# The scan's side projection: the lower contraction half of each unit issued one unit later, and its two partial sums taken by two engines

## The chip, the cores and the metric

The kernel is one program on one core of one Trainium2 chip. The metric is the device time of one execution in microseconds; before the change it is 3687.72 us (median of three runs, 3677.84 to 3689.55). TensorE (PE) multiplies, VectorE (DVE) and ScalarE (ACT) take its results out of the accumulators in PSUM, GpSimd (POOL) helps with masks and stores, SyncE (SP) issues most loads.

## The reference, cut to what matters

The reference is three transformer layers in float32 over 256 latent tokens (and 256 context tokens) of width 2048: an even and an odd attention layer, and a last one with three branches (neighbourhood attention, pooling, an RWKV-7 recurrence), merged by gates. Two parts of the last layer meet in the stage that is changed. One is the recurrence, in both directions of time:

```python
def step(S, inp):
    rt, vt, wt, kt, at, bt = inp
    sa = jnp.einsum('bhij,bhj->bhi', S, at)
    S = S * wt[:, :, None, :] + sa[..., None] * bt[:, :, None, :] + vt[..., None] * kt[:, :, None, :]
    return S, jnp.einsum('bhij,bhj->bhi', S, rt)
```

The other is a plain product: the normed input (256 x 2048) times columns of the layer's input projection, which give the merge gates. It doesn't depend on the recurrence.

## The kernel before, in words

The program is a row of stages, and in each a large projection runs on TensorE beside some other work. Here that stage is `rwkv_scan`, name `scan`.

**The scan** is done in chunks: 16 heads in four groups `g`, each with four steps `s` of 128 tokens, so 16 rounds, the last two steps of each group with outputs ("lat"). Direction `d` is 0 or 1. TensorE makes in each round, for both directions, a fixed row of stages: `turned` (transposes), `products`, `half1`, `level1`, `av`, `half2`, `level2` and so on to `level5` (an inverse by doubling), `tz`, `outer`, `chain1`, `y` (lat only), `chain2`. One stage of one direction is a "visit", `visits` is the list of all 560. Behind most of them another engine works: VectorE adds or transposes (`ft`, `at`, `ak`, `t0`, `y1`, `t1`, ..., `pm`, `m1`, `m2`), ScalarE copies (`ft`, `rb_rk`, `tt0`, `tt1`, `av`, ..., `tz`, `outer`, `y`), GpSimd masks. Each engine has its order written out by loops over the same rounds, and `after` makes an engine wait for another's stage by a counting semaphore.

**The projection beside it** is class `Stream`. Its result is 16 tiles of 128 rows x 512 columns, each a sum over `KD` = 16 slices of 128 contraction rows. One slice is a *unit*: four products of 64 x 64 weights by 512 columns, one in each quadrant of TensorE's array (each is two instructions in the trace, so a unit has 8). Contraction rows 0 to 63 (index `r` = 0, the upper half) add into PSUM bank `ps[0]`, rows 64 to 127 (`r` = 1, the lower) into `ps[1]`. There is one pair of banks. The quadrants are taken in the order (0,0), (1,1), (0,1), (1,0) of (`r`, `o`), `o` being the half of the output rows, so two neighbours differ in both.

**The order.** `units_by(i)` says how many units TensorE has issued before visit `i`: 20 before the first, then shares by the table `share`. In the middle of the stage that is one unit behind each pair of visits of a stage (both directions), two behind `products`. `tiles_by(i)` = `units_by(i) // KD` places `sum_halves(v, t)` on VectorE: ahead of the first stage of VectorE whose visit comes after the tile's last unit. `evict(act, t)` on ScalarE comes six visits later.

When a tile is full, `sum_halves` waits for it and for a free stage buffer, copies `ps[0]` out (L3096), drains, adds `ps[1]` (L3098) and counts `summed`. The first unit of the next tile waits on TensorE for that count:

```python
            if t >= 1:
                pe.wait_ge(self.summed, t)
```

`evict` applies the activation in place (L3105) and issues the store. I call the change from tile `n`-1 to tile `n` *handover `n`*: unit 16`n`-1 ends a tile and unit 16`n` begins the next. There are 15. Where they lie in the order of TensorE, by `units_by`:

| Handover | Last unit issued behind | Visits between | First unit | Visits between | Second unit |
|---|---|---|---|---|---|
| 1 | (lead of 20 units) | none | 16 | none | 17 |
| 2 | level5 | tz | 32 | outer, chain1 | 33 |
| 3 | outer | chain1, chain2 | 48 | turned, products | 49 |
| 4 | chain2 | turned, products (lat) | 64 | none | 65 |
| 5 | products | none | 80 | half1 | 81 |
| 6 | products | half1 | 96 | level1 | 97 |
| 7 | level1 | av, half2 | 112 | level2 | 113 |
| 8 | half2 | level2 | 128 | half3 | 129 |
| 9 | level2 | half3 | 144 | level3 | 145 |
| 10 | half3 | level3 | 160 | half4 | 161 |
| 11 | half4 | level4 | 176 | half5 | 177 |
| 12 | level4 | half5 | 192 | level5 | 193 |
| 13 | half5 | level5 | 208 | tz | 209 |
| 14 | level5 | tz, outer | 224 | chain1, chain2 | 225 |
| 15 | chain1 | y, chain2 | 240 | turned, products | 241 |

SyncE loads weights (quarters of a chunk, six slots) and the scan's inputs; `load_after` decides which weight loads go ahead of which input loads. `store.tile_done` and `store.quarter_read` are counted by TensorE and free the weight slots.

## Time and profile before

| | |
|---|---|
| median of three runs | 3687.72 us (3677.84 to 3689.55) |
| profiled execution, its own time | 3688.84 us |
| its span in the profile | 3687.0 us |
| TensorE busy in the program | 3446.0 us (93%) |
| VectorE busy | 2038.0 us (55%) |
| ScalarE busy | 760.8 us (21%) |
| GpSimd busy | 562.8 us (15%) |
| the scan stage, from its first product to its last sum | 2785.6 to 3344.6 us |
| in it: the projection's 2048 product instructions, busy | 310.6 us, 605 ns mean |
| VectorE's 16 copies / 16 adds of the tiles | 687 / 688 ns mean |
| ScalarE's 16 in-place copies | 630 ns mean |

The span is the profiled execution's own, and lies 1.84 us below its time. Products of TensorE overlap, so a product's own duration is not what a unit costs; that is read from the distance of starts. "idle before" is time in which the engine did nothing, and what ended it.

### The profile page before, as it was taken

The numbers are of one execution on the slowest core, as the hardware profiler recorded it, in microseconds if no ns is written. First come the engines' busy times: TensorE is split into PE (matmuls) and PEld (weight loads), VectorE is DVE, ScalarE is ACT, GpSimd is POOL, SyncE is SP. The second block draws the span as 40 slices with busy tenths as digits, with TensorE's granted clock in tenths as the row PEclk, the third lists the DMA queues.
The fourth block names the chain that finished last, engine by engine and source line by source line (L and its number), as shares of the span: only waits on it lengthen the run. The fifth ranks groups of instructions, "written<-read, shape, count | busy, mean of one in ns | idle before, by whom it ended". The sixth has DMA issues, their size and how long they took to land. (4 is left out here: it accounts for less than half of the span.)

```text
span 3687.0 us, 54760 instructions
## 1 busy us (share of the span) xinstructions
PE 3446.0 (93%) x22059; PEld 1746.9 (47%) x22059; DVE 2038.0 (55%) x3206; ACT 760.8 (21%) x1543; POOL 562.8 (15%) x809
## 2 busy tenths in 40 slices
PE   6999998899989999899989999998899898899998
PEld 2354443334544446454444444454335666664443
DVE  1699992443346867556656647553653444444435
ACT  2100001121320112232110000033552333341000
POOL 0011111121000001100000010252212433432100
PEclk9999999999999999999999999999999999999999
DMA  9988995883245556426466676646875344336763
GB/s 365 346 304 309 355 379 196 321 312 128 74 147 205 182 192 229 167 85 249 167 235 227 245 282 249 240 132 222 279 245 191 114 131 154 118 116 208 238 209 114
DMA packets 362606, 798.66 MB, mean 217 GB/s; under 512 B 26631, under 2 KB 73791, under 8 KB 357747
## 3 DMA queue, kind: packets, MB, share of 16 engines
q1 hardware_dynamic: 259760, 459.54, 36.5%
q0 software_dynamic: 72992, 274.20, 20.7%
q10 hardware_dynamic: 29602, 61.42, 4.4%
q8 instruction: 176, 2.88, 0.3%
q14 instruction: 76, 0.61, 0.0%
HBM read 686.90 MB, written 108.18 MB: 216 GB/s over the span
## 5 line engine op out<-in xcount | busy, mean ns | idle before, releaser
L1228 PE MATMUL gemm_a_g_ps<-store_w,turned 128*128 128x512 f32 (+1 forms) x1152 | 457.2, 559 | 2.7 <-PEq L108 2.7
L759 DVE SCALAR_TENSOR_TENSOR pmods_acc<-pmods_w,cond,pmods_acc 128x512 f32<-128x512 f32 x540 | 384.4, 748 | 23.6 <-issue 0.5
L3084 PE MATMUL scan_g_ps<-store_w,turned 64*64 64x512 f32 x2048 | 310.6, 605 | 19.2 <-DVE outlet_stage L3098 12.3
L1228 PEld LDWEIGHTS gemm_a_g_ps<-store_w,turned 128*128 128x128 f32 x1152 | 209.2, 191 | 250.0 <-issue 250.0
L1228 PE MATMUL att_a_g_ps<-store_w,turned 128*128 128x512 f32 x512 | 240.2, 599 | 6.9 <-ACT outlet_stage L2812 4.2
L1228 PE MATMUL feat_g_ps<-store_w,turned 128*128 128x512 f32 x384 | 181.2, 621 | 15.9 <-ACT outlet_stage L2240 13.7
L1275 PE MATMUL out_c_g_ps<-store_w,turned 128*128 128x512 f32 x384 | 167.6, 592 | 0.0
L1228 PE MATMUL tail_g_ps<-store_w,tail_branch_t 128*128 128x512 f32 x384 | 165.8, 592 | 1.0 <-ACT tail_branch_t L3897 0.9
L1228 PEld LDWEIGHTS att_a_g_ps<-store_w,turned 128*128 128x128 f32 x512 | 91.5, 191 | 100.0 <-issue 93.4
L1228 PEld LDWEIGHTS feat_g_ps<-store_w,turned 128*128 128x128 f32 x384 | 73.2, 197 | 114.9 <-issue 96.0
L1307 DVE TENSOR_TENSOR store_w<-store_w 128x1024 f32<-128x1024 f32 (+1 forms) x108 | 121.1, 1179 | 0.0
L1275 PE MATMUL out_c_g_ps<-out_c_g_form,turned 128*128 128x512 f32 x272 | 118.9, 592 | 0.0
L1275 PEld LDWEIGHTS out_c_g_ps<-store_w,turned 128*128 128x128 f32 x384 | 72.8, 190 | 90.9 <-issue 90.9
L1228 PEld LDWEIGHTS tail_g_ps<-store_w,tail_branch_t 128*128 128x128 f32 x384 | 72.6, 190 | 90.8 <-issue 90.5
L3474 ACT ACTIVATE scan_tmt<-scan_ps 64x256 f32<-64x256 f32 (+1 forms) x224 | 85.1, 380 | 146.3 <-DVE scan_tm L3423 107.4
L1275 PE MATMUL gemm_hq_g_ps<-store_w,turned 128*128 128x512 f32 x256 | 111.2, 592 | 1.8 <-PEq L3972 1.8
L1275 PE MATMUL out_a_g_ps<-store_w,turned 128*128 128x512 f32 (+1 forms) x288 | 112.6, 546 | 0.0
L1275 PE MATMUL out_a_g_ps<-store_w,turned_c 128*128 128x512 f32 (+1 forms) x288 | 112.6, 545 | 0.0
L3084 PEld LDWEIGHTS scan_g_ps<-store_w,turned 64*64 64x64 f32 x2048 | 89.7, 133 | 45.7 <-issue 30.1
L1228 PE MATMUL lat_g_ps<-store_w,lat_turned 128*128 128x512 f32 x224 | 99.5, 603 | 10.8 <-ACT outlet_stage L2420 6.7
L1550 ACT ACTIVATE outlet_stage<-gemm_a_g_ps 128x512 f32<-128x512 f32 (+1 forms) x36 | 20.0, 555 | 433.4 <-PE gemm_a_g_ps L1228 433.4
L3308 PEld LDWEIGHTS scan_ps<-scan_tm,scan_lt 64*64 64x64 f32 x2560 | 77.2, 134 | 46.7 <-POOL scan_lt L3524 24.2
(577 smaller groups left out, 5807.5 us busy)
## 6 DMA issues: line engine op xcount, KB each, us to landing
store_w<-in_w_in SPq DMA_DIRECT2D x160, 1024.0 KB, 7.5
pmods_w<-in_w_mod POOLq DMA_DIRECT2D x40, 2048.0 KB, 13.3
store_w<-in_a_w_in SPq DMA_DIRECT2D x48, 1024.0 KB, 12.5
store_w<-in_c_w_in SPq DMA_DIRECT2D x40, 1024.0 KB, 8.2
first_mods_w<-in_w_mod SPq DMA_DIRECT2D x32, 1024.0 KB, 14.3
store_w<-in_a_w_out SPq DMA_DIRECT2D x32, 1024.0 KB, 6.1
scan_raw<-s_feat SPq DMA_DIRECT2D x112, 256.0 KB, 5.2
s_feat<-feat_o POOLq DMA_DIRECT2D x16, 1536.0 KB, 7.8
```

Source lines behind the costliest of these rows:

```text
L759: v.scalar_tensor_tensor(a, src, x, a, ALU.mult, ALU.add)
L1228: mm = pe.matmul(to, lhs, self.store.slot[i % self.store.NS][:, k, :width], start=first, stop=last)
L1275: mm = pe.matmul(self.pair_bank(n, product, j), act_tile(product, k, j), src[:, kk, :width], start=(k == 0), stop=(k == KT // 2 - 1))
L1307: v.tensor_tensor(w01, w11, w01, ALU.subtract).then_inc(store.piece_made, 1)
L1550: act.activation(outlet.stage[o % 4][:, :w.shape[1]], g.out(t), func).then_inc(copied, 1)
L3084: mm = pe.matmul(self.ps[r][halves[o], :], self.act_tile(k, tb)[halves[r], halves[o]], self.store.slot[i % self.store.NS][halves[r], k % 4 ...
L3308: mm = pe.matmul(quarter(d, 2, 0)[turned_chunk(d, c), h, :], lt[d][chunks[c], k - 1, h, :], tm[d][chunks[c], h, :], start=True, stop=True)
L3474: act.activation(dst, src, ACT.Copy)
```

## The change

TensorE still issues four quadrant products per unit, but the two lower ones are those of the unit before. The new `product(pe, r, o, n)` issues one quadrant product of unit `n`; slot `n` of the order now holds (0,0) of `n`, (1,1) of `n`-1, (0,1) of `n`, (1,0) of `n`-1. Slot 0 has only its two upper products, and the last slot has the two lower products of its own unit behind it. So bank `ps[0]` of a tile is full one slot before bank `ps[1]`.

The handover is split. ScalarE copies `ps[0]` to the stage buffer (`take_upper`) when `upper_done` says that it is full, and counts `upper_taken`; slot 16`n` waits for that. VectorE then only adds `ps[1]` (`sum_halves`) and counts `summed`; slot 16`n`+1 waits for that. `take_upper` stands on ScalarE ahead of the first stage whose visit comes after the tile's last upper products; `sum_halves` on VectorE is placed by `tiles_by` = `(units_by(i) - 1) // KD`, and so is `evict`. `load_after` counts one unit more before a slot of weights is free.

```diff
@@ -3048,7 +3048,8 @@
         self.tiles = [(c, j) for c, job in enumerate(projections) for j in range(len(job[1]))]
         self.out_of = outlet.take(len(self.tiles))
         self.ps = [st.enter_context(nc.psum_tensor(f"{name}_ps{r}", [P, NCH], F32)) for r in range(2)]
-        self.summed, self.evicted = [nc.alloc_semaphore(f"{name}_{s}") for s in ("summed", "evicted")]
+        self.upper_done, self.upper_taken, self.summed, self.evicted = [
+            nc.alloc_semaphore(f"{name}_{s}") for s in ("upper_done", "upper_taken", "summed", "evicted")]
 
     def wait_tile(self, eng, t):
 
@@ -3063,38 +3064,71 @@
         end = begin = self.store.load_of[self.base]
         while end < self.store.load_of[self.base + len(self.projections)] + self.store.NS:
             old, part = (end - self.store.NS - begin) // 4, (end - self.store.NS - begin) % 4
-            if old >= 0 and 2 * KD * old + KD + 4 * (part + 1) > n_units:
+            if old >= 0 and min(2 * KD * old + KD + 4 * (part + 1) + 1, len(self.tiles) * KD) > n_units:
                 break
             end += 1
         self.store.load(sp, end)
 
+    def product(self, pe, r, o, n):
+
+        t, k = n // KD, n % KD
+        c, j = self.tiles[t]
+        i = self.store.load_of[self.base + c] + k // 4
+        halves = (slice(0, HD), slice(HD, P))
+        return pe.matmul(self.ps[r][halves[o], :], self.act_tile(k, self.projections[c][1][j])[halves[r], halves[o]],
+                         self.store.slot[i % self.store.NS][halves[r], k % 4, :], start=(k == 0), stop=(k == KD - 1))
+
     def units(self, pe):
 
-        for t, (c, j) in enumerate(self.tiles):
-            tbs = self.projections[c][1]
-            tb = tbs[j]
-            if t >= 1:
-                pe.wait_ge(self.summed, t)
-            halves = (slice(0, HD), slice(HD, P))
-            for k in range(KD):
-                i = self.store.load_of[self.base + c] + k // 4
-                if j == 0 and k % 4 == 0:
-                    self.store.wait_quarter(pe, i)
-                for r, o in ((0, 0), (1, 1), (0, 1), (1, 0)):
-                    mm = pe.matmul(self.ps[r][halves[o], :], self.act_tile(k, tb)[halves[r], halves[o]],
-                                   self.store.slot[i % self.store.NS][halves[r], k % 4, :], start=(k == 0), stop=(k == KD - 1))
-                if k == KD - 1:
-                    mm.then_inc(self.store.tile_done, 1)
-                elif k % 4 == 3 and j == len(tbs) - 1:
-                    mm.then_inc(self.store.quarter_read, 1)
-                yield
+        def upper_ready(n):
+            t, k = n // KD, n % KD
+            c, j = self.tiles[t]
+            if k == 0 and t >= 1:
+                pe.wait_ge(self.upper_taken, t)
+            if j == 0 and k % 4 == 0:
+                self.store.wait_quarter(pe, self.store.load_of[self.base + c] + k // 4)
+
+        def lower_ready(n):
+            if n % KD == 0 and n >= KD:
+                pe.wait_ge(self.summed, n // KD)
+
+        def upper_finished(mm, n):
+            if n % KD == KD - 1:
+                mm.then_inc(self.upper_done, 1)
+
+        def lower_finished(mm, n):
+            t, k = n // KD, n % KD
+            c, j = self.tiles[t]
+            if k == KD - 1:
+                mm.then_inc(self.store.tile_done, 1)
+            elif k % 4 == 3 and j == len(self.projections[c][1]) - 1:
+                mm.then_inc(self.store.quarter_read, 1)
+        last = len(self.tiles) * KD - 1
+        for n in range(last + 1):
+            upper_ready(n)
+            if n:
+                lower_ready(n - 1)
+            self.product(pe, 0, 0, n)
+            if n:
+                self.product(pe, 1, 1, n - 1)
+            upper_finished(self.product(pe, 0, 1, n), n)
+            if n:
+                lower_finished(self.product(pe, 1, 0, n - 1), n - 1)
+            if n == last:
+                self.product(pe, 1, 1, n)
+                lower_finished(self.product(pe, 1, 0, n), n)
+            yield
+
+    def take_upper(self, act, t):
+
+        self.outlet.wait_free(act, self.out_of + t)
+        act.wait_ge(self.upper_done, t + 1)
+        act.activation(self.stage(t), self.ps[0][:, :], ACT.Copy).then_inc(self.upper_taken, 1)
 
     def sum_halves(self, v, t):
 
-        self.outlet.wait_free(v, self.out_of + t)
+        v.wait_ge(self.upper_taken, t + 1)
         self.wait_tile(v, t)
-        v.tensor_copy(self.stage(t), self.ps[0][:, :])
-        v.drain()
         v.tensor_tensor(self.stage(t), self.stage(t), self.ps[1][:, :], ALU.add).then_inc(self.summed, 1)
 
     def evict(self, act, t):
@@ -3179,9 +3213,13 @@
 
             return lead + (n_units - lead) * room[i // 2] // room[-1]
 
+        def uppers_by(i):
+
+            return units_by(i) // KD
+
         def tiles_by(i):
 
-            return units_by(i) // KD
+            return max(0, units_by(i) - 1) // KD
 
         def mask(d, i):
             return masks[:, d, i, :].unsqueeze(1).broadcast_to([P, HG, HD])
@@ -3501,14 +3539,21 @@
             for k in levels[:-1]:
                 run[f"tt{k}"] = copies(f"level{k}", lambda d, lat, x: swapped(d, tmt[d][:, :, :], quarter(d, 0, 0)), f"t{k}")
             run[f"tt{N_LEVELS}"] = copies(f"level{N_LEVELS}", lambda d, lat, x: [(tmt[d][:, :, :], quarter(d, 0, 0))])
-            t = 0
+            made_by = {"ft": "turned", "rb_rk": "products", "tt0": "products"}
+            t = taken = 0
             for g, s in rounds:
                 for stage in stages("act", steps[s][2]):
                     for d in range(2):
-                        while t < tiles_by(max(0, visit_of[(g, s, {"ft": "turned", "rb_rk": "products", "tt0": "products"}.get(stage, stage.replace("tt", "level")), d)] - 6)):
+                        visit = visit_of[(g, s, made_by.get(stage, stage.replace("tt", "level")), d)]
+                        while taken < uppers_by(visit):
+                            gemm_side.take_upper(act, taken)
+                            taken += 1
+                        while t < tiles_by(max(0, visit - 6)):
                             gemm_side.evict(act, t)
                             t += 1
                         run[stage](d, g, s, steps[s][2])
+            for rest in range(taken, len(gemm_side.tiles)):
+                gemm_side.take_upper(act, rest)
             for rest in range(t, len(gemm_side.tiles)):
                 gemm_side.evict(act, rest)
```

The order of VectorE at handover 4 (round g 0, s 3; `outlet_stage` is the stage buffer, `scan_g_ps` the two banks). Before, the copy and the add stand ahead of the two copies of the transposed inputs (`scan_ft`):

```order
L3438 TENSOR_TENSOR scan_m<-scan_ps,scan_m 64x256 x4
L3096 COPY outlet_stage<-scan_g_ps 128x512
L3098 TENSOR_TENSOR outlet_stage<-outlet_stage,scan_g_ps 128x512
L3397 COPY scan_ft<-scan_ps 128x512 x2
L3402 TENSOR_TENSOR scan_tmt<-scan_ps,scan_masks 128x2x2x64
L3403 TENSOR_TENSOR scan_at<-scan_ps,scan_masks 128x2x2x64
L3402 TENSOR_TENSOR scan_q<-scan_ps,scan_masks 128x2x2x64
L3403 TENSOR_TENSOR scan_at<-scan_ps,scan_masks 128x2x2x64
L3412 TENSOR_TENSOR scan_akt<-scan_ps,scan_masks 128x2x2x64
L3409 STREAM_TRANSPOSE scan_tm<-scan_tmt 128x256
L3412 TENSOR_TENSOR scan_akt<-scan_ps,scan_masks 128x2x2x64
L3409 STREAM_TRANSPOSE scan_tm<-scan_q 128x256
```

Of the change:

```order
L3476 TENSOR_TENSOR scan_m<-scan_ps,scan_m 64x256 x4
L3435 COPY scan_ft<-scan_ps 128x512 x2
L3440 TENSOR_TENSOR scan_tmt<-scan_ps,scan_masks 128x2x2x64
L3441 TENSOR_TENSOR scan_at<-scan_ps,scan_masks 128x2x2x64
L3440 TENSOR_TENSOR scan_q<-scan_ps,scan_masks 128x2x2x64
L3441 TENSOR_TENSOR scan_at<-scan_ps,scan_masks 128x2x2x64
L3450 TENSOR_TENSOR scan_akt<-scan_ps,scan_masks 128x2x2x64
L3447 STREAM_TRANSPOSE scan_tm<-scan_tmt 128x256
L3450 TENSOR_TENSOR scan_akt<-scan_ps,scan_masks 128x2x2x64
L3447 STREAM_TRANSPOSE scan_tm<-scan_q 128x256
L3132 TENSOR_TENSOR outlet_stage<-outlet_stage,scan_g_ps 128x512
L3455 TENSOR_TENSOR scan_y<-scan_ps,scan_eye 128x256 x2
```

The copy is gone, and the add has moved from ahead of `ft` to behind the two transposes `scan_tm` of `t0`: bank `ps[1]` is now full at the end of slot 64, which TensorE issues behind `products`. Slot 65, which follows slot 64 with nothing between, waits on TensorE for this add.

The order of ScalarE at handover 9. The rows are the copies of `av` (`scan_raw`), of level 2 and of level 3 (`scan_tmt`, one row for direction 0 and one for direction 1 each). Before, the projection has its in-place copy behind level 3:

```order
L3474 ACTIVATE scan_raw_0<-scan_ps 128x256
L3474 ACTIVATE scan_raw_1<-scan_ps 64x256 x2
L3474 ACTIVATE scan_tmt<-scan_ps 128x256
L3474 ACTIVATE scan_tmt<-scan_ps 64x256 x2
L3474 ACTIVATE scan_tmt<-scan_ps 128x256
L3474 ACTIVATE scan_tmt<-scan_ps 64x256 x2
L3105 ACTIVATE outlet_stage<-outlet_stage 128x512
L1154 DMA s_merge<-outlet_stage 128x512
```

Of the change:

```order
L3512 ACTIVATE scan_raw_0<-scan_ps 128x256
L3512 ACTIVATE scan_raw_1<-scan_ps 64x256 x2
L3512 ACTIVATE scan_tmt<-scan_ps 128x256
L3512 ACTIVATE scan_tmt<-scan_ps 64x256 x2
L3126 ACTIVATE outlet_stage<-scan_g_ps 128x512
L3512 ACTIVATE scan_tmt<-scan_ps 128x256
L3512 ACTIVATE scan_tmt<-scan_ps 64x256 x2
L3512 ACTIVATE scan_tmt<-scan_ps 128x256
L3512 ACTIVATE scan_tmt<-scan_ps 64x256 x2
```

The new copy out of the bank stands behind the copies of level 2 for both directions and ahead of level 3's.

## Rows read from the trace of the kernel before

**Rows 1.** The page's head.

```profile
span 3687.0 us, 54760 instructions
```

**Rows 2.** Windows: PE, PEld, DVE, ACT, POOL busy, granted clock, DMA; the scan stage.

```profile
2785.00:3345.00 560.00, 503.24 (x13280) 363.02 (x13280) 246.53 (x584) 205.19 (x497) 207.24 (x304) 0.99 0.43 133
```

**Rows 3.** Waits in the scan stage: total us, times, longest.

```profile
PE scan_g_ps L3084 <- DVE outlet_stage L3098: 12.3, 11, 3.4
```

**Rows 4.** Timeline, first handover; start us, us, engine line op.

```profile
2799.68 0.69 DVE L3096 COPY outlet_stage<-scan_g_ps 128x512 f32<-128x512 f32 x1 [4.26 <-PE scan_g_ps L3084]
...
2801.19 2.38 PE L3084 MATMUL scan_g_ps<-store_w,turned 64*64 64x512 f32 x20 [1.64 <-DVE outlet_stage L3098]
```

**Rows 5.** Timeline at handover 10, in level 3 and half 4.

```profile
3121.82 0.75 PE L3308 MATMUL scan_ps<-scan_tm,scan_lt 64*64 64x64 f32 x26
...
3123.26 0.93 PE L3320 MATMUL scan_ps<-scan_tmt,scan_y 64*64 64x64 f32 x32
...
3123.72 0.69 DVE L3096 COPY outlet_stage<-scan_g_ps 128x512 f32<-128x512 f32 x1 [0.47 <-PE scan_g_ps L3084]
...
3125.23 1.09 PE L3084 MATMUL scan_g_ps<-store_w,turned 64*64 64x512 f32 x8 [1.04 <-DVE outlet_stage L3098]
...
3126.14 0.75 PE L3308 MATMUL scan_ps<-scan_tm,scan_lt 64*64 64x64 f32 x26
```

**Rows 6.** Timeline at handover 9, behind level 2.

```profile
3091.36 0.93 PE L3308 MATMUL scan_ps<-scan_tm,scan_lt 64*64 64x64 f32 x32
...
3091.67 0.77 ACT L3474 ACTIVATE scan_tmt<-scan_ps 64x256 f32<-64x256 f32 x2 [0.16 <-issue]
...
3093.33 1.09 PE L3084 MATMUL scan_g_ps<-store_w,turned 64*64 64x512 f32 x8 [1.05 <-DVE outlet_stage L3098]
```

**Rows 7.** Timeline: both copying engines take the two banks of a turned product.

```profile
2868.93 0.60 ACT L3474 ACTIVATE scan_ft<-scan_ps 128x512 f32<-128x512 f32 x1 [5.56 <-PE scan_ps L3269]
2868.93 0.69 DVE L3397 COPY scan_ft<-scan_ps 128x512 f32<-128x512 f32 x1 [1.46 <-PE scan_ps L3269]
```

**Rows 8.** Timeline at handover 2, beside tz.

```profile
2825.79 1.54 PE L3329 MATMUL scan_ps<-scan_raw,scan_tmt 64*64 64x128 f32 x32
...
2826.88 1.89 ACT L3474 ACTIVATE scan_tz<-scan_ps 128x512 f32<-128x512 f32 x3 [0.99 <-PE scan_ps L3329]
...
2827.77 1.09 PE L3084 MATMUL scan_g_ps<-store_w,turned 64*64 64x512 f32 x8 [0.44 <-DVE outlet_stage L3098]
```

**Rows 9.** Timeline at handover 3, between chain 1 and chain 2.

```profile
2865.88 0.95 PE L3359 MATMUL scan_ps<-scan_m,scan_pm 64*64 64x64 f32 x13 [1.34 <-DVE scan_m L3438]
```

**Rows 10.** Timeline behind handover 4: `ft`, last transpose, first unit behind half 1.

```profile
2906.95 1.28 DVE L3397 COPY scan_ft<-scan_ps 128x512 f32<-128x512 f32 x2
...
2911.91 0.45 DVE L3409 STREAM_TRANSPOSE scan_tm<-scan_q 128x256 f32<-128x256 f32 x1
...
2912.91 0.65 PE L3084 MATMUL scan_g_ps<-store_w,turned 64*64 64x512 f32 x2
```

**Rows 11.** Timeline at handover 5, behind products of a first round.

```profile
2946.73 0.84 ACT L3474 ACTIVATE scan_tmt<-scan_q 64x256 f32<-64x256 f32 x2 [3.94 <-DVE scan_tm L3409]
...
2948.10 1.09 PE L3084 MATMUL scan_g_ps<-store_w,turned 64*64 64x512 f32 x8 [3.39 <-DVE outlet_stage L3098]
```

**Rows 12.** Timeline at handover 7, beside av and half 2.

```profile
3014.19 0.77 ACT L3474 ACTIVATE scan_tmt<-scan_ps 64x256 f32<-64x256 f32 x2 [0.16 <-issue]
...
3015.86 1.09 PE L3084 MATMUL scan_g_ps<-store_w,turned 64*64 64x512 f32 x8 [0.47 <-DVE outlet_stage L3098]
```

**Rows 13.** Timeline from the stage's end to the next stage's first product.

```profile
3344.66 0.63 ACT L3105 ACTIVATE outlet_stage<-outlet_stage 128x512 f32<-128x512 f32 x1 [3.38 <-DVE outlet_stage L3098]
...
3346.84 3.75 PE L1275 MATMUL tail_g_ps<-store_w,turned 128*128 128x512 f32 x4 [3.79 <-PEq L3972]
```

**Rows 14.** Windows round two long idle stretches of TensorE (columns of Rows 2).

```profile
2940.00:2950.00 10.00, 6.48 (x137) 3.80 (x133) 7.16 (x17) 1.60 (x4) 9.09 (x15) 1.00 0.29 81
...
3066.00:3072.00 6.00, 6.00 (x138) 4.73 (x139) 0.00 (x0) 2.54 (x5) 0.00 (x0) 0.72 0.16 49
```

## The prediction

> **What bounds the kernel now.** I read the page's head first: the span is 3687.0 us [rows 1], and the profiled execution's own time is 3688.84 us, 1.1 above the median of 3687.72. Then the stretch of the scan stage, the only one that the change touches: in 560 us TensorE is busy for 503.2, VectorE for 246.5, ScalarE for 205.2 [rows 2]. So the stage is TensorE's, and both other engines have room; what they do costs time only where TensorE waits for it. Third the waits: the projection's units stand idle for 12.3 us, 11 times, until VectorE's add [rows 3]. That is the wait that the change splits. Last the timeline at each handover, for what it costs and what would come in its place.
>
> The plain case is handover 10 [rows 5]. From one pair of visits to the next, with one unit between, it is 3123.26 - 3121.82 = 1.44 us. Across the handover it is 3126.14 - 3123.26 = 2.88. So a handover costs 1.44 us. A unit alone takes 3126.14 - 3125.23 = 0.91, hence a pair of visits 0.53. The copy starts 0.46 after the last unit's end (3123.72 against 3123.26, where TensorE goes on), and the unit starts at 3125.23, 0.05 after copy and add (0.69 each, 0.08 between) have ended. The wait's length is latency and serial work, 0.46 + 0.69 + 0.08 + 0.69 + 0.05 = 1.97, less the 0.53 of visits that cover it.
>
> **The change, part by part.** It removes 16 copies and drains on VectorE and adds 16 copies on ScalarE. VectorE and ScalarE start on the banks of one turned product at the same 2868.93 and take 0.69 and 0.60 [rows 7], so I give the new copy 0.60 and the same 0.46 and 0.05 round it. ScalarE's path is then 0.46 + 0.60 + 0.05 = 1.11 us from the unit's end (*upper wait*), and VectorE's 0.46 + 0.69 + 0.05 = 1.20 from the end of the next slot (*lower wait*). Both are longer than the 0.53 of one pair of visits. The single wait of 1.44 becomes two: 1.11 - 0.53 = 0.58, then 1.20 - 0.53 = 0.67. That is the point of the forecast: two short paths, each with its own latency, stand one behind the other, since in most of the stage one slot lies between two pairs of visits. By handover:
>
> - 8, 10, 11 (last unit behind a half): 0.58 + 0.67 = 1.25 against 1.44, -0.2 each, -0.6.
> - 9, 12 (behind a level): ScalarE must first finish the level's copies, from 3091.67 for 0.77 to 3092.44 [rows 6]; the new copy stands behind them (the order of ScalarE above), ends at 3093.1, and the slot starts at 3093.15 against 3093.33 now. It gains 0.2, the lower wait adds 0.67: +0.5 each, +1.0.
> - 13: upper wait 0.58; the lower is covered by tz, a pair that takes about 1.97 - 0.8 = 1.2 (next line). 0.6 against 1.44: -0.8.
> - 2: the unit starts at 2827.77, where the path of 1.97 from 2825.79 ends [rows 8]. TensorE's idle time there is 0.44, to which the tail of the last modelled product adds some 0.36, so the cost is 0.8. ScalarE's copy would run from 2826.25 to 2826.85, beside tz, and be out of the way as ScalarE's own tz copy starts at 2826.88. Both waits go: -0.8.
> - 3: the sum stands ahead of `m1`, and chain 2 waits 1.34 for it [rows 9]; both halves of it now lie where TensorE has other work: -1.3.
> - 14: free now. The add moves between `pm` and `m1`, behind slot 224; `m1` can start 1.15 after that slot (0.46 + 0.69) in place of about 0.28 + 0.41 = 0.69 (half a pair of visits, and the latency): +0.5.
> - 15: covered before and after, 0.
> - 4: the new order's worst place. The add, now behind `t0`, holds slot 65. The last transpose ends at 2911.91 + 0.45 = 2912.36 [rows 10]; as the sum no longer holds up `ft` (2906.95), all of it comes some 0.4 earlier (0 to 0.69 possible). Add and latency end at 2912.7, slot 65 at 2913.6, the pair of half 1 at 2914.1, where it now ends at 2912.91: +1.2.
> - 5: the unit waits 3.39 us now, and starts at 2948.10 [rows 11]. ScalarE's copy stands behind its `tt0`, which ends at 2946.73 + 0.84 = 2947.57; plus 0.03, 0.60 and 0.05 is 2948.25, +0.15. Then the lower wait, +0.67. +0.8. Handover 6 has the same order behind `products`: +0.8.
> - 7: ScalarE's copy follows 3014.19 + 0.77 = 3014.96 and lets the slot start at 3015.6 against 3015.86 [rows 12], -0.25; lower wait +0.67: +0.4.
> - 1: no visits between. 1.97 now (2801.19 less 2799.68 is 1.51, plus the 0.46) [rows 4]; 1.11 + 1.20 after: +0.35.
>
> Sum: -0.6 + 1.0 - 0.8 - 0.8 - 1.3 + 0.5 + 1.2 + 0.8 + 0.8 + 0.4 + 0.35 = +1.55.
>
> **The ends.** Slot 0 holds half a unit and takes at most a whole one's time, so the lead of 20 slots doesn't grow (it may lose 0.45). At the end the two lower products of unit 255 stand alone, 0.45 to 0.9. TensorE isn't what ends the stage: its next product starts at 3346.84, after ScalarE's last in-place copy from 3344.66 [rows 13]. From unit 255's end that chain has 0.46 + 0.69 + 0.08 + 0.69 = 1.92 now; then 0.9 + 0.46 + 0.69 = 2.05, the upper copy being done beside. +0.1.
>
> **What else moves.** The 11 us of copies (16 x 0.69) that leave VectorE buy nothing by themselves, as it is idle for over half of the stage [rows 2]; where its queue counted (3, 4) it is priced above. ScalarE gets 16 x 0.60 = 9.6 us; behind `take_upper` stand its own stage copies. In the plain rows these are due two stages later, and at handover 2 the copy fits in the gap by 0.03; were that gone it would cost 0.1. Freed weight slots come one slot later, and no unit waits for weights in the waits of this stage; SyncE's rule shifts by the same one, so its input loads aren't held. The products are the same 2048.
>
> Total +1.65 us on 3688.84 is 3690.5; against the median, 3687.72 + 1.65 = **3689.4 us**. A measurement of this kernel can tell about 0.3% (11 us) from no change; this is 0.04%. Each latency has bounds: were ScalarE's path 0.3 shorter or longer at 15 handovers, the sum would run from -3 to +6.
>
> **Rivals.**
>
> *Both waits hidden.* If ScalarE and VectorE each got their bank out under the visits, all of what handovers cost now would go: six of 1.44, 1.97, 0.8, 1.3, 0.4, 3.4, 0.9 and 0.85, some 18 us: 3670. For it: both engines are idle for over half of the stage. Against it: 1.11 and 1.20 against a cover of 0.53. 0.06. Here the Trainium skill speaks for the change: "TensorEngine Tiling (Array Packing)", section PSUM Bottleneck, advises to use ScalarE and VectorE both to empty PSUM. By it the time would be this rival's. The rows show a wait made of latencies, not of throughput.
>
> *More waits, lower clock (slower).* Where TensorE idles, its clock may fall to the lower level. Behind an idle stretch that ended at 3065.96 it shows 0.72 of full over 6 us [rows 14], so 1.7 us lost; but round the 3.39 us ahead of unit 80 it stayed at 1.00, and the stage has 0.99 with its 11 waits [rows 2, 11, 14]. About 12 lower waits are new. From six such falls on (6 x 1.7 = 10, with the 1.65) it is slower by over 0.3%; all 12 give 3689.4 + 20 = 3710. 0.05. The Trainium skill has this as a rule, "TensorE: Matmul & The Clock Gate", section on psum-queue depth-cycling: a kernel that cycles through PSUM banks with short idle times between groups makes the clock swing. The trace disagrees so far, by that 0.99.
>
> *Quadrants that no longer read the same slice (slower).* Neighbouring products of a slot now stream slices of two units. No row shows such a pair. If it cost 0.04 us a unit, 256 x 0.04 = 10 us would decide; a unit whose four quadrants ran one by one would double to 1.8, +230. The nearest row is the unit itself, which already streams from different partitions for the two halves, so I take 0. 0.03.
>
> *Drift.* The three runs lie 11.7 us apart, and the instructions behind the edit move in memory; TensorE's idle stretches that no engine released are in the same stage. Within the range; a little of it lies beyond 0.3% on either side, 0.03 and 0.03.
>
> **How the numbers follow.** Forecast and drift within 0.3%: 0.80, plus 0.01 for the clock case in its mild form. Faster 0.09 (0.06 + 0.03), slower 0.10 (0.04 + 0.03 + 0.03). The range is the forecast with the spread of the runs, 13 below and 11 above: 3676 to 3700; the two far cases lie outside.
>
> **What would show it.** In the profile after: ScalarE's 16 new copies at 0.60 us; TensorE's units waiting for ScalarE at some 11 handovers (0.6 us, longest 3.4 at handover 5) and again for VectorE at some 11 (0.7, longest about 2.7 at handover 4); no wait of chain 2 at handover 3; a stage of 560 us within 3; a granted clock of 0.99. A pair-to-pair distance other than 1.44 away from handovers would show the quadrant rival, a lower clock the second, and units that wait for VectorE less than 4 us in all the first.

## The result, and the profile after

The changed kernel takes 3692.18 us (median of 20 runs, 3685.30 to 3696.23), the kernel before 3685.07 (20 runs, 3677.84 to 3696.25). The ratio is 1.0018, with a 95% interval of 1.0012 to 1.0024: slower by 4.4 to 8.8 us. I had forecast +1.65. One execution of the kernel before in the comparisons told below took 6304.35 us at a granted clock of 0.677; the ratios leave it out.

The page's head of the kernel after (the profiled execution's own time is 3691.34 us):

```profile
span 3689.6 us, 54760 instructions
```

Its windows, of the same 560 us (columns as in [rows 2]):

```profile
2785.00:3345.00 560.00, 502.17 (x13207) 364.46 (x13205) 234.38 (x565) 213.26 (x510) 203.38 (x298) 0.98 0.42 130
```

Against [rows 2] VectorE has lost 12 us (234.38 for 246.53) and ScalarE gained 8 (213.26 for 205.19), about what 16 instructions of 0.69 and 0.60 make. TensorE gets 1 us less done in the same stretch, and its granted clock is 0.98 for 0.99.

The waits of TensorE there (columns as in [rows 3]):

```profile
PE scan_g_ps L3078 <- ACT outlet_stage L3126: 7.6, 7, 3.7
...
PE scan_g_ps L3078 <- DVE outlet_stage L3132: 3.2, 2, 2.3
```

12.3 us in 11 waits [rows 3] have become 7.6 in 7 for ScalarE and 3.2 in 2 for VectorE, 10.8 in all. The sum of waits fell by 1.5 us and the time rose. Short waits are missing from this view, since they hide under a product's modelled end (handover 10, below, shows no idle time). So I also went by starts.

The view of the stage buffer, with how long its instructions take (ns: shortest, median, longest):

```profile
L3126 ACT ACTIVATE outlet_stage<-scan_g_ps x15: 597/597/599, 2795.7 to 3307.9; 128x512 f32<-128x512 f32 x15
L3132 DVE TENSOR_TENSOR outlet_stage<-outlet_stage,scan_g_ps x15: 649/689/689, 2797.6 to 3311.1; 128x512 f32<-128x512 f32 x15
```

The new copy takes 0.60 us, as I had put it.

The timeline at handover 10, which answers to [rows 5]:

```profile
3123.99 0.90 PE L3346 MATMUL scan_ps<-scan_tm,scan_lt 64*64 64x64 f32 x27
...
3125.59 0.92 PE L3358 MATMUL scan_ps<-scan_tmt,scan_y 64*64 64x64 f32 x32
...
3125.96 0.60 ACT L3126 ACTIVATE outlet_stage<-scan_g_ps 128x512 f32<-128x512 f32 x1 [0.89 <-PE scan_g_ps L3078]
...
3126.61 1.09 PE L3078 MATMUL scan_g_ps<-store_w,turned 64*64 64x512 f32 x8
...
3127.52 0.93 PE L3346 MATMUL scan_ps<-scan_tm,scan_lt 64*64 64x64 f32 x32
...
3127.84 0.69 DVE L3132 TENSOR_TENSOR outlet_stage<-outlet_stage,scan_g_ps 128x512 f32<-128x512 f32 x1 [0.79 <-PE scan_g_ps L3078]
...
3128.58 1.09 PE L3078 MATMUL scan_g_ps<-store_w,turned 64*64 64x512 f32 x8
...
3129.49 0.75 PE L3358 MATMUL scan_ps<-scan_tmt,scan_y 64*64 64x64 f32 x26
...
3130.94 0.75 PE L3346 MATMUL scan_ps<-scan_tm,scan_lt 64*64 64x64 f32 x26
```

Away from the handover, pair to pair is 3130.94 - 3129.49 = 1.45 us, as before (1.44). Slot 160 starts 1.02 after the end of the unit ahead (3126.61 - 3125.59), and slot 161 1.97 after slot 160 (3128.58 - 3126.61), where 1.45 would be no wait. From pair 3125.59 to pair 3129.49 it is 3.90 for two slots, 1.00 more than 2 x 1.45. Before, the one slot with the handover took 2.88, 1.44 too much. So this handover gains 0.4, where I had -0.2.

The timeline at handover 4, which answers to [rows 10]:

```profile
2902.19 1.04 PE L3078 MATMUL scan_g_ps<-store_w,turned 64*64 64x512 f32 x8
...
2904.50 0.45 DVE L3447 STREAM_TRANSPOSE scan_tm<-scan_q 128x256 f32<-128x256 f32 x1
...
2904.86 0.65 DVE L3132 TENSOR_TENSOR outlet_stage<-outlet_stage,scan_g_ps 128x512 f32<-128x512 f32 x1
...
2905.57 1.09 PE L3078 MATMUL scan_g_ps<-store_w,turned 64*64 64x512 f32 x8 [2.34 <-DVE outlet_stage L3132]
```

The add stands behind the last transpose, and slot 65 waits 2.34 us for it, as forecast (3.38 from start to start; 0.86 before).

At handover 5 ([rows 11] before), the first execution of the kernel after:

```profile
2938.49 1.04 PE L3078 MATMUL scan_g_ps<-store_w,turned 64*64 64x512 f32 x8
...
2941.08 0.45 DVE L3447 STREAM_TRANSPOSE scan_tm<-scan_q 128x256 f32<-128x256 f32 x1 [0.16 <-POOL scan_q L3568]
2941.56 0.84 ACT L3512 ACTIVATE scan_tmt<-scan_q 64x256 f32<-64x256 f32 x2 [3.94 <-DVE scan_tm L3447]
...
2942.56 0.60 ACT L3126 ACTIVATE outlet_stage<-scan_g_ps 128x512 f32<-128x512 f32 x1 [0.16 <-issue]
...
2943.21 1.99 PE L3078 MATMUL scan_g_ps<-store_w,turned 64*64 64x512 f32 x8 [3.67 <-ACT outlet_stage L3126]
...
2944.97 1.30 PE L3346 MATMUL scan_ps<-scan_tm,scan_lt 64*64 64x64 f32 x28
...
2945.33 0.69 DVE L3132 TENSOR_TENSOR outlet_stage<-outlet_stage,scan_g_ps 128x512 f32<-128x512 f32 x1 [3.80 <-PE scan_g_ps L3078]
```

ScalarE stands idle from 2937.6 to 2941.56 (3.94, for VectorE's transpose), and the copy stands behind `tt0`, though the bank was full some 3 us earlier (slot 79 starts at 2938.49 and takes 1.04). Slot 80 starts after 3.67 us of idle time, where [rows 11] had 3.39. Then something the sum did not have: its eight products take 1.99 us, where they took 1.09 in [rows 11]. That is the lower level of the clock, 1.2 GHz (the granted clock stands below). The same at handover 6:

```profile
2978.58 0.84 ACT L3512 ACTIVATE scan_tmt<-scan_q 64x256 f32<-64x256 f32 x2 [4.61 <-DVE scan_tm L3447]
...
2979.58 0.60 ACT L3126 ACTIVATE outlet_stage<-scan_g_ps 128x512 f32<-128x512 f32 x1 [0.15 <-issue]
...
2980.23 1.99 PE L3078 MATMUL scan_g_ps<-store_w,turned 64*64 64x512 f32 x8 [0.74 <-ACT outlet_stage L3126]
...
2982.35 0.69 DVE L3132 TENSOR_TENSOR outlet_stage<-outlet_stage,scan_g_ps 128x512 f32<-128x512 f32 x1 [2.39 <-PE scan_g_ps L3078]
```

The idle time just ahead is only 0.74 (TensorE had stood idle for 0.55 and 0.35 us more in the 3 us before it), and the products again take 1.99. The windows of the kernel after round both places (in the kernel before, [rows 14] has 1.00 round handover 5):

```profile
2943.00:2949.00 6.00, 5.79 (x116) 3.67 (x118) 2.24 (x5) 0.80 (x3) 5.57 (x9) 0.74 0.01 3
2977.00:2983.00 6.00, 4.36 (x70) 2.67 (x68) 2.83 (x7) 1.43 (x3) 6.00 (x10) 0.77 0.73 255
```

The same for the kernel before:

```profile
2948.00:2954.00 6.00, 5.90 (x164) 4.11 (x165) 2.34 (x7) 1.94 (x6) 5.75 (x9) 1.00 0.21 61
2981.00:2987.00 6.00, 5.74 (x160) 4.02 (x162) 3.08 (x9) 2.91 (x7) 5.93 (x9) 1.00 0.77 249
```

The granted clock, third from the end, is 0.74 and 0.77 after, 1.00 and 1.00 before.

The other waits that the prediction named: chain 2 at handover 3, 1.34 us before [rows 9]. In the waits of TensorE after, its line has left

```profile
PE scan_ps L3397 <- DVE scan_m L3476: 0.7, 3, 0.2
```

so that wait is gone, as forecast.

**All fifteen.** For each handover `n` the time from the start of slot 16`n`-1 to that of slot 16`n`+2 holds both waits. Of two profiled executions of the kernel before, three of the changed one, and four of variants told below:

```
handover   sum had   before         changed               early_h5 early_h6 copy_early skew_vector
 1         +0.35     4.47   4.47    5.12   5.12   5.12     5.12    5.12     5.12      5.23
 2         -0.8     10.36  10.36    9.68   9.69   9.69     9.68    9.68     9.69      9.68
 3         -1.3      9.92  11.54    8.81   8.81   8.81     8.81    8.81     8.81      9.14
 4         +1.2      8.71   8.72    9.82   9.82   9.82     9.82   10.65     9.82     11.04
 5         +0.8      7.32   8.94    9.02   9.38  10.27     5.22    9.35     5.22      7.08
 6         +0.8      7.24   7.24    9.20   9.17   8.04     8.04    7.06     7.05      7.06
 7         +0.4      5.78   5.78    6.21   6.21   6.21     6.21    6.21     6.21      5.59
 9         +0.5      5.78   5.78    6.21   6.21   6.21     6.21    6.21     6.21      5.51
10         -0.2      5.77   5.76    5.35   5.35   5.35     5.35    5.35     5.35      5.45
11         -0.2      5.77   5.78    5.40   5.40   5.40     5.40    5.40     5.40      5.51
15          0        8.86   8.86    8.86   8.86   8.86     8.86    8.86     8.86      8.93
```

Handovers 8, 12, 13 and 14 are left out: idle stretches of 1 to 3 us that no engine releases fall into them in some executions. Together they take 38.7 and 39.0 us before and 37.7, 38.7 and 40.0 in the changed kernel, the same in the mean. The nine quiet rows (all here but 5 and 6) sum to 65.44 in the first execution of the kernel before and 65.47 to 65.48 in the changed one: +0.03, where my terms give -0.05. The second execution of the kernel before has 67.05, since its clock fell at handover 3 (11.54 for 9.92); the 10.65 and 11.04 at handover 4 have a fall too. Rows 5 and 6 sum to 14.56 and 16.18 before, 18.22, 18.55 and 18.31 after: +3.0 between the means, where I had +1.6.

### The profile page after: what moved, and what is told of

Its sections match the earlier page's. It is cut to its first block and busy times, and to the rows that moved or that the text cites. A ratio compares the mean times of both kernels' runs of the same rounds, so it can differ in the third digit from the quotient of the medians.

```text
span 3689.6 us, 54760 instructions
## 1 busy us (share of the span) xinstructions
PE 3449.3 (93%) x22059; PEld 1751.7 (47%) x22059; DVE 2027.6 (55%) x3190; ACT 770.2 (21%) x1559; POOL 562.8 (15%) x809
## 3 DMA queue, kind: packets, MB, share of 16 engines
q8 instruction: 176, 2.88, 0.3%
## 5 line engine op out<-in xcount | busy, mean ns | idle before, releaser
L1228 PE MATMUL lat_g_ps<-store_w,lat_turned 128*128 128x512 f32 x224 | 100.5, 608 | 10.8 <-ACT outlet_stage L2420 6.7
```

Of the source, the lines that this page charges most:

```text
L1228: mm = pe.matmul(to, lhs, self.store.slot[i % self.store.NS][:, k, :width], start=first, stop=last)
```

## The experiments

Three groups of runs, each with the kernel before in turn on the same chip, whose medians there were 3686.78 (35 runs), 3685.90 (27) and 3688.06 (35).

**First group: is it the order, the second engine, or the two waits?**

*again*: the changed kernel once more, with no edit.

> The changed kernel once more, for a second profile beside the first. In the first its scan stage lasts 569.5 us against 561.3 before, of which 3.3 us lie at the handovers' two slots and 4.9 us elsewhere: more stretches in which TensorE stands idle with no engine behind it, and six falls of its granted clock in place of two. If these belong to the changed kernel, the stage is again 567 to 571 us, with five or more falls at the same slots; if they are chance of one execution, they lie at other slots and the stage may be 563 to 566 us. Against before: slower by 4 to 9 us, as the twenty runs have it.

Measured: 3693.18 us (12 runs), ratio 1.0015 (1.0006 to 1.0024). The loss repeats. The stage took 568.7 us with seven falls of the clock, and four of the first profile's six stand at the same slots (handovers 5 and 6, slots 120 and 254): in part the kernel's, in part chance.

*before_no_handover*: the kernel before, whose TensorE never waits at a handover. Copy and add read other data of the same size, so the projection's result doesn't reach the output.

```diff
-            if t >= 1:
-                pe.wait_ge(self.summed, t)
...
-        v.tensor_copy(self.stage(t), self.ps[0][:, :])
+        v.tensor_copy(self.stage(t), self.read[:, 0:NCH])
...
-        v.tensor_tensor(self.stage(t), self.stage(t), self.ps[1][:, :], ALU.add).then_inc(self.summed, 1)
+        v.tensor_tensor(self.stage(t), self.stage(t), self.read[:, NCH:2 * NCH], ALU.add).then_inc(self.summed, 1)
```

> The kernel before, with VectorE's copy and add reading from SBUF in place of the two banks, and TensorE never waiting for them; loads of all engines stay. It prices all 15 handovers. By my sum they cost 18 us (six of 1.44, 1.97, 0.8, 1.3, 0.4, 3.4, 0.9, 0.85): faster than before by 15 to 20 us. If handovers only shift idle time that TensorE would have anyway, under 8 us.

Measured: 3676.37 us (12 runs), ratio 0.9969 (0.9959 to 0.9979).

*after_no_handover*: the same with the changed kernel, both waits gone.

```diff
-            if k == 0 and t >= 1:
-                pe.wait_ge(self.upper_taken, t)
...
-            if n % KD == 0 and n >= KD:
-                pe.wait_ge(self.summed, n // KD)
+            return
...
-        act.activation(self.stage(t), self.ps[0][:, :], ACT.Copy).then_inc(self.upper_taken, 1)
+        act.activation(self.stage(t), self.read[:, 0:NCH], ACT.Copy).then_inc(self.upper_taken, 1)
...
-        v.tensor_tensor(self.stage(t), self.stage(t), self.ps[1][:, :], ALU.add).then_inc(self.summed, 1)
+        v.tensor_tensor(self.stage(t), self.stage(t), self.read[:, NCH:2 * NCH], ALU.add).then_inc(self.summed, 1)
```

> The changed kernel with both its handover waits and its reads of the banks taken away in the same manner (ScalarE and VectorE still work on data in SBUF). Theory 1, the loss is in the waits and what they do to the clock: this kernel equals the one before without handovers within 2 us. Theory 2, the loss is in the changed order of the products itself or in how the instructions reach TensorE: it is 4 to 6 us slower than that one.

Measured: 3675.78 us (12 runs), ratio 0.9975 (0.9963 to 0.9987). Without handovers the changed order is not slower (0.9969 and 0.9975, intervals that overlap). So streaming two slices in one slot costs nothing that shows within the some 4 us that these runs can tell, and the loss comes with the handovers. Taking all handovers away gains some 10 us net in the kernel before, and not the 18 that I had put in the first rival. Where the handover holds nothing up, TensorE meets VectorE, whose copy and add still stand ahead of the scan's own work, one stage later: in before_no_handover slot 161 comes 2.24 us after slot 160 (1.45 in the kernel before), since a transpose stands behind copy and add. The waits of TensorE there have a line for such transposes, which the kernel before doesn't have:

```profile
PE scan_ps L3307 <- DVE scan_tm L3422: 3.3, 3, 2.6
```

The 10 us is a rough price, for the copy that reads the other data is not the old one. It takes 0.43 us in place of 0.69, and 2.51 once, at handover 8, which makes the 2.6 in that line:

```profile
L3094 DVE COPY outlet_stage<-turned x16: 426/429/2509, 2797.9 to 3333.4; 128x512 f32<-128x512 f32 x16
```

In after_no_handover one add takes 4.93 us (at 3013.71), and TensorE waits 4.11 for the transpose behind it. What stretched the two was not tested. That profile is also of the slowest of its 12 executions, 3689.92 us.

*both_copy*: the kernel before without the skew; ScalarE copies the upper bank to the stage buffer and VectorE the lower one to a buffer of its own, at the same time, and the add comes two stages later from there.

```diff
             if t >= 1:
-                pe.wait_ge(self.summed, t)
+                pe.wait_ge(self.upper_taken, t)
+                pe.wait_ge(self.lower_taken, t)
...
+        act.activation(self.stage(t), self.ps[0][:, :], ACT.Copy).then_inc(self.upper_taken, 1)
...
+        v.tensor_copy(self.lower[:, :], self.ps[1][:, :]).then_inc(self.lower_taken, 1)
...
+        v.tensor_tensor(self.stage(t), self.stage(t), self.lower[:, :], ALU.add).then_inc(self.summed, 1)
```

> The kernel before (no skew), but at a handover ScalarE copies the upper bank to the stage buffer while VectorE copies the lower one to a buffer of its own in SBUF, and the add comes two stages later from SBUF. TensorE's path is then 0.46 + the longer of 0.60 and 0.69 + 0.05 = 1.20 us in place of 1.97: 0.77 less at handovers behind a half or without cover, 0.2 less behind a level, where ScalarE comes 1.1 us late. Sum about -7 us against before: faster by 4 to 9 us. If the clock or idle time elsewhere takes it back, within 2 us of before.

Measured: 3686.60 us (12 runs), ratio 0.9999 (0.9989 to 1.0009); the 4 to 9 us that I expected didn't come. A plain handover is shorter (10: 4.97 us in place of 5.77 before), but handover 5 takes 9.20, since ScalarE's copy stands behind `tt0` there too and the clock falls behind it. The waits show both:

```profile
PE scan_g_ps L3087 <- ACT outlet_stage L3099: 7.0, 6, 3.7
...
PE scan_g_ps L3087 <- DVE scan_g_lower L3104: 1.2, 2, 0.9
```

**Second group: ScalarE's place in its queue.** A new theory: the loss is at handovers 5 and 6, where `take_upper` stands behind `tt0`.

*copy_early*: the changed kernel with the copy ahead of `tt0` at these two.

```diff
-                        while taken < uppers_by(visit):
+                        early = visit_of[(g, s, "products", 1)] + 1 if stage in ("rb_rk", "tt0") else visit
+                        while taken < uppers_by(early):
```

> The changed kernel with one thing moved: at handovers 5 and 6 ScalarE's copy of the upper bank stands ahead of its tt0 copies in place of behind them. If the part of the loss that I had not priced (about 4 to 5 us of some 6.5) comes from these two places, where TensorE's clock fell in both profiles of the changed kernel: no fall of the clock at them, slots 80 and 81 together in 4 us in place of 6.7 to 7.6, and 3 to 5 us less than the changed kernel, so 1 to 4 us slower than before. If they play no part beyond their waits in the trace: about 2.5 us less. If the loss lies elsewhere: unchanged, 5 to 7 us slower than before.

Measured: 3686.82 us (11 runs), ratio 1.0001 (0.9992 to 1.0010). The loss is gone, with two of ScalarE's 1559 instructions moved. By its rows 5 and 6 (12.27 us, for 14.56 and 16.18 before) the kernel should even be faster than the one before, by some 3 us, and it isn't; that is taken up under what stays open.

*skew_vector*: the changed kernel with its order and its two waits, but VectorE takes both banks.

```diff
-        act.activation(self.stage(t), self.ps[0][:, :], ACT.Copy).then_inc(self.upper_taken, 1)
+        v.tensor_copy(self.stage(t), self.ps[0][:, :]).then_inc(self.upper_taken, 1)
...
+                    while taken < uppers_by(visit_of[(g, s, made_by.get(stage, stage), d)]):
+                        while t < taken:
+                            gemm_side.sum_halves(v, t)
+                            t += 1
+                        gemm_side.take_upper(v, taken)
+                        taken += 1
```

> The changed kernel's order of products and its two waits, but VectorE does both, the copy of the upper bank and the add of the lower; ScalarE is as before. If ScalarE's lateness matters (behind a level 0.6 us each at handovers 9 and 12, and at 5 and 6 its tt0 copies, 0.8 each) this is 3 to 4 us faster than the changed kernel; behind a half it is 0.1 slower each. If only the number of waits in a row matters, it equals the changed kernel within 1 us.

Measured: 3686.14 us (11 runs), ratio 1.0001 (0.9992 to 1.0010). Two waits as such don't cost the 6 us either. VectorE's copy at handover 5 lets slot 80 start after 2.62 us of idle time, since it doesn't stand behind `tt0`, and its products take 1.09:

```profile
2943.91 0.65 DVE L3126 COPY outlet_stage<-scan_g_ps 128x512 f32<-128x512 f32 x1
...
2944.62 1.09 PE L3078 MATMUL scan_g_ps<-store_w,turned 64*64 64x512 f32 x8 [2.62 <-DVE outlet_stage L3126]
```

*both_early*: both_copy with the two early places.

```diff
-                    while t < tiles_by(visit_of[(g, s, made_by.get(stage, stage), d)]):
+                    early = visit_of[(g, s, made_by.get(stage, stage), d)] + ((stage, d) == ("ak", 1))
+                    while t < tiles_by(early):
                         gemm_side.take_lower(v, t)
...
-                        while taken < tiles_by(visit):
+                        early = visit_of[(g, s, "products", 1)] + 1 if stage in ("rb_rk", "tt0") else visit
+                        while taken < tiles_by(early):
```

> The kernel in which both engines copy a bank each, with both copies of handovers 5 and 6 placed earlier (ScalarE's ahead of tt0, VectorE's ahead of the second ak). Slot 80 starts 1.5 us earlier and slot 96 about 0.5: 2 us faster than both_copy, so 2 us faster than before where that one was equal, and up to 8 if the whole gain worked out for it came. If TensorE gives the gain back by waiting for its own instructions, again within 1 us of before.

Measured: 3684.19 us (11 runs), ratio 0.9995 (0.9987 to 1.0004). The lowest median of all complete kernels, but not to be told from the kernel before.

*before_again*: the kernel before, for a second profile.

> The kernel before, for a second profile. Theory: with its one wait per handover its clock does not fall at handovers 5 and 6, and its stage lasts 559 to 564 us with two to four falls in all. If a fall stands at one of them here too, those falls are chance and not the change's.

Measured: 3686.97 us, span 3685.0. It moved my reading. Handover 5 takes 8.94 us here and 7.32 in the first profile; ahead of it TensorE is idle for 3.40 us (first profile 3.39), and this time the clock falls:

```profile
2948.31 1.58 PE L3084 MATMUL scan_g_ps<-store_w,turned 64*64 64x512 f32 x8 [3.40 <-DVE outlet_stage L3098]
```

```profile
2948.00:2954.00 6.00, 5.69 (x100) 3.58 (x102) 1.89 (x5) 0.38 (x1) 5.96 (x9) 0.72 0.01 3
```

0.72, where the first profile has 1.00 in the same stretch. The 1.00 in [rows 14], on which the prediction leaned, was one of two outcomes.

**Third group: the two places apart.**

*early_h5* and *early_h6*: copy_early for handover 5 alone and for 6 alone (`(g, s)` = (1, 0) and (1, 1)).

```diff
-                        early = visit_of[(g, s, "products", 1)] + 1 if stage in ("rb_rk", "tt0") else visit
+                        early = visit_of[(g, s, "products", 1)] + 1 if (g, s) == (1, 0) and stage in ("rb_rk", "tt0") else visit
```

> The changed kernel with ScalarE's copy of the upper bank ahead of tt0 at handover 5 alone. Theory: the loss is the local one at these two handovers. From the starts in the profiles, slots 80 to 82 took 4.71 + 1.97 + 2.70 = 9.38 us in the changed kernel and 1.80 + 1.97 + 1.45 = 5.22 with the copy early, 4.2 less; so this kernel is about 4 us below the changed one, ratio to the kernel before 1.0006 to 1.0009. Slot 80 starts 1.8 us behind slot 79, and slot 82 1.45 behind slot 81. Rival (the two matter only together, by the clock that falls at both): no gain or the whole one, 1.0017 or 1.0001. Rival (what copy_early gained was how its build happened to lie in memory): nothing follows the number of copies moved, any value from 0.9995 to 1.002.

> The changed kernel with ScalarE's copy of the upper bank ahead of tt0 at handover 6 alone. Theory: slots 96 and 97 took 4.04 + 2.87 us in the changed kernel and 2.91 + 2.11 with the copy early, 1.9 less; so this kernel is about 2 us below the changed one, ratio to the kernel before 1.0011 to 1.0013, and handover 5 shows its 4.71 and the half clock behind it as before. Rival (only together): 1.0017 or 1.0001. Rival (memory): any value from 0.9995 to 1.002, in no order with early_h5.

*copy_early_again* and *changed_third*, with no further edit:

> Copy_early once more, in the same call as its two halves. Theory: ratio to the kernel before 1.0000 to 1.0004, 6 us below the changed kernel, and the stage without a fall of the granted clock at handovers 5 and 6. Rival (chance): above 1.0010.

> The changed kernel in the same call as the three above: ratio 1.0015 to 1.0020, slots 80 and 96 at 4.71 and 4.04 us behind the slot before, granted clock fallen at both places. The gains of early_h5 and early_h6, taken from this run, should add up to that of copy_early_again, about 4 + 2 = 6 us.

Measured, 12 runs each: changed_third 3690.06 us, ratio 1.0011 (0.9999 to 1.0022); early_h6 3689.23, 1.001 (1.0 to 1.002); early_h5 3685.70, 1.0 (0.999 to 1.001); copy_early_again 3686.07, 0.9997 (0.9985 to 1.0008). From the changed kernel's median that is -0.8, -4.4 and -4.0 us. By the table's rows 5 and 6 the three should gain 1.9 (early_h6, 16.41 for a mean of 18.36), 5.1 (early_h5, 13.26) and 6.1 (12.27). Moving the copy at handover 5 alone takes the loss away, so the rival by which both places matter only together falls. The rival of memory is left with little: of the changed kernel's own order, the two programs with that copy moved (copy_early, twice, and early_h5) are level with the kernel before, and the two with it behind `tt0` (the changed kernel, three times, and early_h6) are not. For handover 6 the slots show about 1.0 of gain without the clock and the time can't tell it from 0; that the two gains add up was not shown. The changed kernel's own ratio is at the low end here: -0.4 to 8.1 us, where the first two comparisons have 4.4 to 8.8 and 2.2 to 8.8.

Handover 5 of early_h5:

```profile
2943.00 1.04 PE L3078 MATMUL scan_g_ps<-store_w,turned 64*64 64x512 f32 x8
...
2944.16 0.60 ACT L3126 ACTIVATE outlet_stage<-scan_g_ps 128x512 f32<-128x512 f32 x1 [2.03 <-PE scan_g_ps L3078]
...
2944.80 1.09 PE L3078 MATMUL scan_g_ps<-store_w,turned 64*64 64x512 f32 x8 [0.76 <-ACT outlet_stage L3126]
...
2946.03 0.69 DVE L3132 TENSOR_TENSOR outlet_stage<-outlet_stage,scan_g_ps 128x512 f32<-128x512 f32 x1
2946.07 0.84 ACT L3512 ACTIVATE scan_tmt<-scan_q 64x256 f32<-64x256 f32 x2 [1.32 <-DVE scan_tm L3447]
```

```profile
2944.00:2950.00 6.00, 5.24 (x136) 3.57 (x134) 3.95 (x10) 2.36 (x6) 6.00 (x10) 1.00 0.32 96
2977.00:2983.00 6.00, 5.13 (x134) 3.51 (x136) 2.35 (x7) 3.04 (x8) 6.00 (x9) 1.00 0.74 235
```

The copy starts soon after the bank is full, slot 80 waits 0.76 us in place of 3.67, `tt0` (2946.07) isn't held up, and the clock stays at 1.00 at both handovers.

## Why the prediction was right, and where it was not

"Within 0.3%" held, and the kernel landed in the range. The size did not: +1.65 against 4.4 to 8.8. Of the signs that I had set, two failed: the stage was to take 560 us within 3 and took 569.5, 568.7 and 565.9 (561.3 and 559.5 before), and the granted clock of 0.99 was 0.98.

**Pair to pair away from handovers** stayed at 1.45. The quadrant rival, slower by mixed slices, didn't come: by that distance, and by the two kernels without handovers.

**The two waits one behind the other** (the point of the forecast) is what the timeline shows. The sizes were a little high: I had 0.58 and 0.67 for upper and lower, and measured 1.93 - 1.45 = 0.48 and 1.97 - 1.45 = 0.52. The latency that I took from the old handover, 0.46, is 0.37 for ScalarE (3125.96 - 3125.59) and 0.32 for VectorE (3127.84 - 3127.52) in the rows of handover 10. Hence -0.4 for 10 and 11, not -0.2. Behind a level, 9 and 7, +0.43 each against +0.5 and +0.4.

**Handovers 1, 2, 3, 4, 15**: +0.65, -0.68, -1.11, +1.11 and 0, against +0.35, -0.8, -1.3, +1.2 and 0. At 1 the two waits don't follow the sum by 0.3; the rest is right within 0.2. Handovers 8, 12, 13 and 14 can't be read off single executions; their sum is unchanged, as forecast (-0.2 + 0.5 - 0.8 + 0.5 = 0).

**The step that failed: handovers 5 and 6, "+0.8 each"**, through the clock. Where the clock doesn't fall, 0.8 is right for both, in part by luck: the upper wait grew by 0.28 (4.71 for 4.43 at 5, 4.04 for 3.76 at 6) where I had 0.15, the lower is 0.52 where I had 0.67. At 6 the third execution of the changed kernel has 8.04 against 7.24. At 5, slot 80 starts 4.71 after slot 79 in all three (before 4.43), and slot 81 follows 1.97 us behind it where the clock holds; with 1.45 for slot 82 that is 8.13 against 7.32. But the clock fell at handover 5 in all three executions (and in early_h6, with the same 3.67 us of idle time), and at 6 in two of the three, which makes 8.13 into 9.02 to 10.27 and 8.04 into 9.2. In the kernel before it fell at 5 in one execution of two, 7.32 into 8.94, and at 6 in neither. That is 2.2 us against 0.8 between the means, +1.4, the whole of the gap between +1.6 and +3.0. The prediction priced the clock at nothing there: "round the 3.39 us ahead of unit 80 it stayed at 1.00". The rival "more waits, lower clock" came true in this mild form, to which I gave 0.01. I had priced a fall at 1.7 us; at these two places one cost 0.9 to 2.1. Its strong form, a fall at each of 12 new lower waits, did not come: the slots behind the short waits at 7, 9, 10 and 11 keep their lengths in every execution. Up to the next stage's first product I count 6, 7 and 4 falls in the changed kernel against 3 and 4 before, but the 12 that don't stand at handovers 5 and 6 all go with idle stretches of 1.4 to 3.5 us that no engine releases. The new wait of 2.34 us at handover 4, which I had priced at the full clock too, was followed by a fall in three of the eight executions that have it, though in none of the changed kernel's three. In early_h6:

```profile
2909.68 1.58 PE L3078 MATMUL scan_g_ps<-store_w,turned 64*64 64x512 f32 x8 [2.35 <-DVE outlet_stage L3132]
```

The Trainium skill has the rule in "TensorE: Matmul & The Clock Gate", section "A second HAM failure mode: psum-queue depth-cycling", by which frequent short idle times between groups of products make the clock go to and fro. The runs agree with it at most at handover 6, where the clock fell behind short idle times in two of five executions (0.74 us just ahead of slot 96, in the changed kernel, early_h5 and both_copy); skew_vector waits as often at handovers (10 times in the waits of its stage, against 9 after) and keeps 1.00 at both places, as its windows say:

```profile
2944.00:2950.00 6.00, 5.24 (x142) 3.57 (x144) 2.70 (x6) 1.94 (x5) 6.00 (x10) 1.00 0.18 51
2978.00:2984.00 6.00, 5.80 (x161) 3.89 (x154) 3.21 (x8) 2.94 (x8) 6.00 (x9) 1.00 0.87 291
```

**The ends**: the first slot takes 0.45 us in place of 0.88, which I had as possible and not in the sum; from the last slot to the next stage's first product it is 5.06, 5.06 and 5.35 in the changed kernel's three executions (before 4.92 and 4.91), +0.15 or +0.4 against +0.1.

**Both waits hidden** stayed far off: 10.8 us of handover waits are left. The sign that I had set for this rival, less than 4 us of waiting for VectorE, did show (3.2 in the view), but it was a bad sign: by the distances of starts TensorE waits some 0.5 us for VectorE at plain handovers, and the view hides that under the modelled ends of products. The Trainium skill's advice for this change ("TensorEngine Tiling (Array Packing)", section PSUM Bottleneck: let ScalarE and VectorE both empty PSUM) is not borne out here: both_copy does it, at 0.9999. With the engine's place in its queue mended as well, both_early has 0.9995, still no difference.

**What stays open.** The runs show what the copy's place at handover 5 is worth: 4.4 us between changed_third and early_h5. They don't show that the whole loss lay there. Against the kernel before, rows 1 to 7, 9 to 11 and 15 cost 3.0 us, by the first two comparisons the change costs 4.4 to 8.8 and 2.2 to 8.8, and handovers 8 and 12 to 14 cost nothing in the mean. So by the first comparison 1.4 to 5.8 us lie elsewhere in the stage. From the start of slot 1 to that of slot 255, the 15 handovers and the rest take (us, one number for each profiled execution):

```
                 the 15 handovers        the rest
before           118.7  122.3            436.7  431.4
changed          121.4  122.8  123.8     442.6  440.5  436.4
early_h5         116.0                   433.7
early_h6         120.1                   436.9
copy_early       117.2  114.8            433.8  440.7
skew_vector      118.2                   438.1
both_copy        116.8                   440.9
both_early       113.3                   440.8
```

All variants but early_h6 are level with the kernel before in time, though their handovers take 0.5 to 5.4 us less than in the better of its two executions. Where their rest is longer, that gives the gain back; but the rest scatters by 5 us and more between executions of one kernel, so what takes the gain wasn't settled. Part of the rest is idle time that no engine releases: in the waits of TensorE from 2785 to 3345 us the lines that end in "issue" sum to 26.5 and 23.8 us before, 33.0, 30.4 and 31.0 in the changed kernel, and 29.4 and 29.1 in the two profiles of copy_early, which is not slower. A profile's stage alone doesn't carry a difference of 3 us. The profiled executions' own times are 3691.34, 3690.76 and 3688.72 us of the changed kernel and 3688.84 and 3686.97 of the one before, 2.4 apart in the mean.

## What to carry to other kernels

When a drain is split over two engines, look up for each handover what stands ahead of the copy in the second engine's queue: here one copy stood behind an instruction that itself waited (`tt0`), and moving it ahead gave back 4.4 us, about the size of the loss. A split drain pays its latency twice when only one group of other work lies between the halves. And a wait taken away at one place need not shorten the whole: both_early has the shortest handovers and the time of the kernel before. Where TensorE already idles for some microseconds, one profile with a full clock behind it is one draw: price the lower level too.
